# A 64-byte step between the first block of each weight piece and the rest

## The reference, cut to what matters

```python
def swiglu(h, w_in, w_out):
    gu = jnp.einsum('bld,de->ble', h, w_in)
    g, u = jnp.split(gu, 2, axis=-1)
    return jnp.einsum('blf,fd->bld', jax.nn.silu(g) * u, w_out)

# first block, per layer, for x and (but for the last layer) for the context
q, k, v, up, ca, cb = project_inputs(h, w_in[l], q_norm_g[l], k_norm_g[l])
mix = jnp.concatenate([attn, pool_o, conv_o], axis=-1)
x = x + g1 * jnp.einsum('blm,md->bld', mix, w_out[l])
x = x + g2 * swiglu(modulate(rms_norm(x, norm2_g[l]), sh2, sc2), w_ffn_in[l], w_ffn_out[l])
# second block, per layer
c_q, c_kv, k_r, q_d, k_d, v_d = jnp.split(h @ w_in[l], split_at, axis=-1)
x = x + mixed @ w_out[l]
x = x + conv_ffn(rmsnorm(x, ffn_norm[l]), w_up[l], conv_w[l], conv_b[l], w_down[l])
```

## Time and profile before

| | |
|---|---|
| median of 3 runs | 1796.46 us |
| lowest, highest | 1794.70, 1797.76 us |
| the profiled execution | 1794.97 us |
| its span, first to last instruction | 1793.1 us |
| mean granted TensorE clock | 0.977 |
| TensorE matmul busy, weight load busy | 1685.8 us (94%), 1526.0 us (85%) |
| VectorE, ScalarE, GpSimd busy | 1063.0 us (59%), 886.3 us (49%), 192.7 us (11%) |
| weights and other input read | 296.10 MB, mean 166 GB/s |

### The profile page before, as it was taken

The page is one execution under the profiler, slowest core; times in us unless marked ns, Lnnn a source line. Parts: engine busy times, 40 slices in busy tenths (PEclk is TensorE's granted clock), DMA queues, the critical chain, the costliest instruction groups (busy, mean ns, idle before and its releaser), DMA issues. The chain is left out here.

```text
span 1793.1 us, 30262 instructions
## 1 busy us (share of the span) xinstructions
PE 1685.8 (94%) x12864; PEld 1526.0 (85%) x12864; DVE 1063.0 (59%) x1472; ACT 886.3 (49%) x1192; POOL 192.7 (11%) x138
## 2 busy tenths in 40 slices
PE   5899988999999999997999999988999999889999
PEld 2777666999999999965899989757999987679999
DVE  2498657644445444986644445755776456657773
ACT  3334555544345434555544335655555366556552
POOL 1140000122003210300022100000011000000110
PEclk7899999999999999999999999999999999999999
DMA  9233646466446545363266453302555533025553
GB/s 368 94 141 136 240 165 216 184 235 252 171 165 211 185 174 182 141 238 138 99 221 201 172 174 130 132 22 86 186 184 194 177 120 134 24 95 184 184 195 119
DMA packets 45110, 299.12 MB, mean 167 GB/s; under 512 B 5216, under 2 KB 7360, under 8 KB 11696
## 3 DMA queue, kind: packets, MB, share of 16 engines
q1 hardware_dynamic: 44304, 295.65, 46.0%
q0 software_dynamic: 240, 0.79, 0.1%
q10 hardware_dynamic: 432, 0.75, 0.1%
HBM read 296.10 MB, written 1.06 MB: 166 GB/s over the span
## 5 line engine op out<-in xcount | busy, mean ns | idle before, releaser
L1749 DVE TENSOR_TENSOR wl<-raw,wh 128x2048 fp32r<-128x2048 f32 (+3 forms) x236 | 529.0, 2242 | 520.8 <-ACT wh L1523 470.0
L1523 ACT ACTIVATE wh<-raw 128x2048 fp32r<-128x2048 f32 (+3 forms) x236 | 436.8, 1854 | 259.4 <-PE bank L1334 158.8
L1329 PE MATMUL bank<-hx_hi,wh 128*128 128x256 f32 x1920 | 547.9, 285 | 16.3 <-ACT hx_hi L1523 9.7
L1332 PE MATMUL bank<-hx_hi,wl 128*128 128x256 f32 x1920 | 539.8, 281 | 3.3 <-DVE wl L1749 3.3
L1334 PE MATMUL bank<-hx_lo,wh 128*128 128x256 f32 x1920 | 540.4, 281 | 0.0
L1329 PEld LDWEIGHTS bank<-hx_hi,wh 128*128 128x128 f32 x1920 | 364.0, 190 | 23.9 <-issue 19.7
L1332 PEld LDWEIGHTS bank<-hx_hi,wl 128*128 128x128 f32 x1920 | 364.3, 190 | 8.8 <-DVE wl L1749 4.6
L1334 PEld LDWEIGHTS bank<-hx_lo,wh 128*128 128x128 f32 x1920 | 363.8, 189 | 0.5 <-DVE hx_lo L1741 0.2
L1332 PE MATMUL bank<-hid_hi,wl 128*128 128x256 f32 x880 | 245.4, 279 | 0.5 <-DVE wl L1749 0.5
L1334 PE MATMUL bank<-hid_lo,wh 128*128 128x256 f32 x880 | 245.4, 279 | 0.0
L1329 PE MATMUL bank<-hid_hi,wh 128*128 128x256 f32 x880 | 245.3, 279 | 0.0
(11 more groups left out here) (208 smaller groups left out, 1955.0 us busy)
## 6 DMA issues: line engine op xcount, KB each, us to landing
raw<-in_wts SPq DMA_DIRECT2D x258, 1024.0 KB, 4.8
raw<-in_wts SPq DMA_DIRECT2D x20, 768.0 KB, 4.0
raw<-in_wts SPq DMA_DIRECT2D x4, 576.0 KB, 3.5
tmp<-tscr SPq DMA_DIRECT2D x16, 128.0 KB, 4.3
raw<-in_wts SPq DMA_DIRECT2D x2, 640.0 KB, 3.9
xTc<-in_ctxT SPq DMA_DIRECT2D x1, 1024.0 KB, 10.8
xTx<-in_xT SPq DMA_DIRECT2D x1, 1024.0 KB, 8.6
out_x<-xTx POOLq DMA_DIRECT2D x3, 256.0 KB, 5.5
```

The source lines that it names most:

```text
L1329: pe.matmul(out, hi[:, k, c:c + m], x_hi, start=first and k == 0 and o == 0, stop=False, skip_group_check=True)
L1332: pe.matmul(out, lo[:, k, c:c + m], x_hi, start=False, stop=False, skip_group_check=True)
L1523: return act.activation(out, in_, func, bias=bias, scale=scale)
L1749: tt(M.wl[k][:, 0:ne], M.raw[f["r"]][:, 0:ne], M.wh[k][:, 0:ne].bitcast(F32), ALU.subtract).then_inc(*on.inc(f["tlo"]))
```

## The change

Every piece whose operands are read block by block gets 16 columns of zeros (64 bytes) behind its first block. `wh` and `wl` start at a multiple of 128 bytes. Block 0 thus starts at a multiple of 128, and every later block 64 bytes behind one, as all blocks did before. `mod` and `ukv` pieces get no step and so lie at multiples of 128 throughout. A slot grows to 2064 columns, 8256 bytes. The eight small tensors `st` (32 bytes each) move into the 64-byte gaps that alignment leaves between the `wh` and `wl` buffers. The three `raw` buffers lie behind each other without alignment, so the middle one now starts 64 bytes behind a multiple of 128. The loads, the splits by ScalarE and VectorE and the input array carry the 16 columns along. The matmuls are the same in number, order and shape; they never read the zeros.

```diff
+STEP = 16
-SLOT = 2048
+SLOT = 2048 + STEP
...
-        keys += [(("up1", l, j), SLOT) for j in range(22)]
+        keys += [(("up1", l, j), 2048, 256) for j in range(22)]
...
-    return {k: (i, n) for i, (k, n) in enumerate(keys)}
+    return {k: (i, n + STEP if first else n, first) for i, (k, n, first) in enumerate(keys)}
...
         def align(at):
-            cur[0] += (at - cur[0]) % 256
+            cur[0] += (at - cur[0]) % 128
...
-        align(192)
-        self.wh = [sb(f"wh{i}", [P, SLOT], F32R) for i in range(NSPLIT)]
-        self.wl = [sb(f"wl{i}", [P, SLOT], F32R) for i in range(NSPLIT)]
+        self.wh, self.wl, self.st = [], [], []
+        for i in range(2 * NSPLIT):
+            align(0)
+            w, name = ((self.wh, "wh"), (self.wl, "wl"))[i % 2]
+            w.append(sb(f"{name}{i // 2}", [P, SLOT], F32R))
+            if i < 4:
+                self.st += [sb(f"st{2 * i + j}", [P, 8]) for j in range(2)]
...
+    def block(w, k, ncols, c, m):
+        at = k * ncols + (STEP if k else 0) + c
+        return w[:, at:at + m]
...
-                pe.matmul(out, hi[:, k, c:c + m], x_hi, start=first and k == 0 and o == 0, stop=False,
+                pe.matmul(out, block(hi, k, ncols, c, m), x_hi, start=first and k == 0 and o == 0, stop=False,
...
-                pe.matmul(out, a[0][:, k, sl], hi[:, k, :], start=k == 0 and j == 0, stop=False, skip_group_check=True)
+                pe.matmul(out, a[0][:, k, sl], block(hi, k, 256, 0, 256), start=k == 0 and j == 0, stop=False, skip_group_check=True)
...
     def put(key, a):
-        row, n = PT[key]
-        out[row, :, 0:n] = a
+        row, n, first = PT[key]
+        if first:
+            out[row, :, 0:first], out[row, :, first + STEP:n] = a[:, 0:first], a[:, first:]
+        else:
+            out[row, :, 0:n] = a
```

More of the change, by code:

```diff
@@ L31, in piece_table @@
         for cb in range(3):
-            keys += [(("mod", l, cb, k), SLOT) for k in range(8)]
-        keys += [(("in1", l, j), SLOT) for j in range(9)]
-        keys += [(("out1", l, kh, ch), SLOT) for kh in range(2) for ch in range(2)]
-        keys += [(("up1", l, j), SLOT) for j in range(22)]
-        keys += [(("dn1", l, ch, kb), (2048, 2048, 1536)[kb]) for ch in range(4) for kb in range(3)]
-    for l in range(2):
[L38 to L43, removed]
-    return {k: (i, n) for i, (k, n) in enumerate(keys)}
+            keys += [(("mod", l, cb, k), 2048, 0) for k in range(8)]
+        keys += [(("in1", l, j), 2048, 256) for j in range(9)]
+        keys += [(("out1", l, kh, ch), 2048, 512) for kh in range(2) for ch in range(2)]
+        keys += [(("up1", l, j), 2048, 256) for j in range(22)]
+        keys += [(("dn1", l, ch, kb), (2048, 2048, 1536)[kb], 256) for ch in range(4) for kb in range(3)]
+    for l in range(2):
+        keys += [(("in2", l, 2), 1280, 160) if j == 2 else (("in2", l, j), 2048, 256) for j in range(9)]
+        keys += [(("uq", l, j), 1152, 384) for j in range(2)]
+        keys += [(("ukv", l), 2048, 0)]
+        keys += [(("out2", l, kh, ch), 2048, 512) for kh in range(2) for ch in range(2)]
+        keys += [(("up2", l, j), 2048, 256) for j in range(22)]
+        keys += [(("dn2", l, ch, kb), (2048, 2048, 1536)[kb], 256) for ch in range(4) for kb in range(3)]
+    return {k: (i, n + STEP if first else n, first) for i, (k, n, first) in enumerate(keys)}
 def vec_table():
@@ L199, in __init__ @@
         self.nlam = sb("nlam", [P, 2])
-        self.st = [sb(f"st{i}", [P, 8]) for i in range(8)]
         self.tmp = [sb(f"tmp{i}", [P, 512]) for i in range(8)]
@@ L286, in dma @@
             r = n % NRAW
-            row, ne = self.PT[self.pieces[n]]
+            row, ne, _ = self.PT[self.pieces[n]]
             t = self.ev(f"raw{r}", 16)
@@ L1318, in tensor_program @@
 def tensor_program(pe, on, M, plan):
+    def block(w, k, ncols, c, m):
+        at = k * ncols + (STEP if k else 0) + c
+        return w[:, at:at + m]
     def gemm(f, nk, ncols, tiles, a, a_toks, k0, first, last, free, t, **_):
-        hi = M.wh[f["k"]][:, 0:nk * ncols].rearrange("p (k c) -> p k c", k=nk)
-        lo = M.wl[f["k"]][:, 0:nk * ncols].rearrange("p (k c) -> p k c", k=nk)
+        hi, lo = M.wh[f["k"]], M.wl[f["k"]]
         for k in range(nk):
@@ L1328, in gemm @@
                     on.wait_ge(free[j])
-                pe.matmul(out, hi[:, k, c:c + m], x_hi, start=first and k == 0 and o == 0, stop=False,
+                pe.matmul(out, block(hi, k, ncols, c, m), x_hi, start=first and k == 0 and o == 0, stop=False,
                           skip_group_check=True)
                 on.wait_ge(f["tlo"])
-                pe.matmul(out, lo[:, k, c:c + m], x_hi, start=False, stop=False, skip_group_check=True)
+                pe.matmul(out, block(lo, k, ncols, c, m), x_hi, start=False, stop=False, skip_group_check=True)
                 on.wait_ge(a_toks[k0 + k][1])
-                ins = pe.matmul(out, hi[:, k, c:c + m], x_lo, start=False, stop=last and k == nk - 1,
+                ins = pe.matmul(out, block(hi, k, ncols, c, m), x_lo, start=False, stop=last and k == nk - 1,
                                 skip_group_check=True)
@@ L1338, in gemm_tok @@
     def gemm_tok(f, nk, b, free, a, a_toks, t, **_):
-        hi = M.wh[f["k"]][:, 0:nk * 256].rearrange("p (k c) -> p k c", k=nk)
-        lo = M.wl[f["k"]][:, 0:nk * 256].rearrange("p (k c) -> p k c", k=nk)
+        hi, lo = M.wh[f["k"]], M.wl[f["k"]]
         on.wait_ge(free, f["thi"])
@@ L1345, in gemm_tok @@
                 on.wait_ge(a_toks[k][0])
-                pe.matmul(out, a[0][:, k, sl], hi[:, k, :], start=k == 0 and j == 0, stop=False, skip_group_check=True)
+                pe.matmul(out, a[0][:, k, sl], block(hi, k, 256, 0, 256), start=k == 0 and j == 0, stop=False, skip_group_check=True)
                 on.wait_ge(f["tlo"])
-                pe.matmul(out, a[0][:, k, sl], lo[:, k, :], start=False, stop=False, skip_group_check=True)
+                pe.matmul(out, a[0][:, k, sl], block(lo, k, 256, 0, 256), start=False, stop=False, skip_group_check=True)
                 on.wait_ge(a_toks[k][1])
-                ins = pe.matmul(out, a[1][:, k, sl], hi[:, k, :], start=False, stop=k == nk - 1, skip_group_check=True)
+                ins = pe.matmul(out, a[1][:, k, sl], block(hi, k, 256, 0, 256), start=False, stop=k == nk - 1, skip_group_check=True)
         ins.then_inc(*on.inc(t))
@@ L1461, in mla_k1 @@
     def mla_k1(hp, f, b, free, ck_toks, t, **_):
-        whi, wlo = (x[f["k"]][:, :].rearrange("p (k c) -> p k c", k=2) for x in (M.wh, M.wl))
+        whi, wlo = (x[f["k"]][:, 0:2048].rearrange("p (k c) -> p k c", k=2) for x in (M.wh, M.wl))
         on.wait_ge(free, f["thi"], f["tlo"])
```

## The result

The changed kernel takes 1783.32 us (median of 4 runs, 1781.76 to 1784.55) beside 1797.11 us before (4 runs): ratio 0.9918, 95% interval 0.9905 to 0.9931, 13.8 us less. The profiled execution took 1783.53 us, its span is 1781.6 us; against the 1794.97 us of before, that is 11.4 us less. The prediction had 1767 us.

The account below looks back on a forecast made before the run. TensorE's pace of starting matmuls in the long stages was taken as the bound. 1794.97 - 25.2 - 5.5 + 1.0 = 1765.3 us for the profiled execution, 1766.8 at the median, rounded to 1767; range 1753 to 1811.

Parts of the forecast that it names:

- The rule on SBUF: TensorE's operand reads: by the skill page no address could change the matmul pace, the change slightly slower for its columns.
- the first rival: Matmul pace: addresses don't matter or nudges cancel, leaving 1 us for the columns, 1797.5 us; no effect within 0.2%, chance 0.14.
- The step as a nudge: Entry to each piece and after block 0: the address shift leads long-paced matmuls into the short pace; 30.7 us won.
- second rival: Entry into block 1: nudge brings the long pace, 5.9 us lost, block 0 slower, 7 us; 1810 us, chance 0.28.
- The third rival: Split pieces: the step works only in part, for instance not behind stalls; half of 30.7 us, 1782 us, chance 0.13.
- The 28.8 us for 2180 triples at full effect: Saturated long-paced stages: each group of three matmuls shortens by 0.0132 us; 25.2 us won with block 0 left long.
- Block 0 was charged with the long pace: First block of each piece: assumed to stay at the long pace, so 28.8 x 7/8 = 25.2 us.
- The short-paced pieces: Stretches already at the short pace, 446 triples: no loss in the main sum, 5.9 us lost if all turned long.
- The mixed stages: Stages with attention and modulation among projections, 948 triples: half of 12.5 x 7/8, 5.5 us won.
- The columns: Splits and loads carrying 16 more columns: 14 ns on ScalarE, 18 ns on VectorE; together 1 us lost, range 0 to 3.
- The DMA rule: Loads at a pitch of 8256 bytes: misaligned rows cost 261 beats on the mean instead of 256, hidden at DMA share 0.5.
- The cover: Feeding of TensorE at the shorter pace, 5.44 us a piece: loads and splits keep up, nothing becomes late.

Follow-up runs that it names:

- e1_front: Changed kernel with the zeros moved ahead of block 0, so no step within a piece; 1776.76 us, ratio 0.9876 to the kernel before.
- e2_zero: Changed kernel with the zeros moved behind the piece, so all blocks of split pieces lie at multiples of 128; 1817.86 us, ratio 1.0104 to the kernel before.
- f3_step: Changed kernel with alignment kept modulo 256: the step in the old layout, small tensors filling gaps; 1804.22 us, ratio 1.0039 to the kernel before.
- g2_distance: Kernel before with only the three `wh` buffers moved, by 128 bytes down, to 64 modulo 256; 1774.37 us, ratio 0.9874.
- g1_both: Kernel before, no zeros, with activations moved to 128 and `wl` to 64 modulo 256, `wh` staying at 192; 1772.76 us, ratio 0.9857.
- g4_distance_same: Kernel before with activations staying at 0 and `wh` and `wl` both at 64 modulo 256; 1779.83 us, ratio 0.9896.
- g3_turned: Kernel before with activations at 128, `wh` at 64 and `wl` at 192 modulo 256; 1785.71 us, ratio 0.9945.
- f1_halves: Kernel before with `wl` alone moved by 128, to 64 modulo 256, `wh` staying at 192; 1789.59 us, ratio 0.9946.
- f2_moving: Kernel before with the activations alone moved from 0 to 128 modulo 256; 1778.00 us, ratio 0.9894.

## Why the prediction failed in its main step and held in others

**What bounds the kernel.** Right: the pace in the long stages. Addresses alone moved the time from 1776.76 us in `e1_front` to 1817.86 in `e2_zero`, which have the same work, loads and splits.

**The rule on SBUF.** The Trainium skill, "SBUF — State Buffer", section "SBUF: two separate sides", has it that TensorE never waits on anyone in SBUF, by which no address would matter (the first rival, 1797.5). The measurements say otherwise: 1.0104 in `e2_zero` and 0.9876 in `e1_front`, which differ only in where the weights lie within the same buffers. The page may mean waits on other engines only. Whether it is reads of TensorE against each other, no run shows.

**The step as a nudge.** This is what failed. The prediction had the step lead the stream from the long pace into the short one at equal addresses. `f3_step`, the step alone, does the opposite: +7 us. And in the new layout it costs 6.6 us (`e1_front`). Its second rival described the step alone: the short stretches are gone. Its price was too high, 5.9 + 7 us and 1 for the columns against 7 measured in all.

**The sign and the number.** That the kernel got faster as forecast, though by 13.8 us and not by 29, is luck: the forecast had it from the step, and it came from the layout. The third rival had 1782 us for a partial effect, close to the measured 1783.32, and that is luck too. It had the step work in some pieces and fail in those behind a stall. In the long stages of the trace every piece, behind a stall or not, has the short pace in its bulk and pays at its entry.

**What was overlooked.** The sentence that everything "keeps its remainder modulo 128" was true and the wrong question. `align` modulo 128 moves the activations by 128 modulo 256 and sets `wh` and `wl` 128 apart. That side effect is the whole gain: it makes the distance pair (64, 192), at which only the short pace lasts. `g2_distance` makes the same pair by moving `wh` alone.

**The size of the terms.** The 28.8 us for 2180 triples at full effect are right for the pace alone: `g1_both`, with the short pace throughout, gains 27.3 in its even distances. Its stages get only 19.5 shorter. Block 0 was charged with the long pace in 2 of 16 triples, 0.026 us a piece; it costs 0.079, as the passage reaches into block 2. That makes 0.132 x 2180 / 16 = 18.0 us instead of 25.2. The even distances show 17.7 and the stages 12.9. The 4.9 us between them go at waits and at the lower clock, 2.0 of them from 300 to 350 us; one by one the rest isn't assigned. The short-paced pieces, at 0 in the forecast, lose 0.079 x 446 / 16 = 2.2 us, and the three stages show 2.2. The mixed stages were to bring 5.5 us and brought 0.9 with the columns in it; even `g1_both`, with neither step nor columns, gets only 3.6 there. Half of their ceiling was too much: other engines and the clock (0.97 to 0.95 from 696 to 875 us) set the time there. 12.9 - 2.2 + 0.9 is 11.6, and 0.1 is lost from 885 to 896 us: 11.4 us (unrounded), the difference of the profiled executions.

**The columns.** Right: 15 and 17 ns a split where 14 and 18 were expected. A `ukv` piece has 60 matmuls where the prediction said about 72, a term that it took as nothing either way.

The DMA rule of the Trainium skill, "DMA: Bandwidth & Descriptors", section "How a descriptor splits into AXI transactions", would make the loads at a pitch of 8256 bytes slower. The prediction's estimate from that page, 261 beats instead of 256, would be 4.85 us instead of 4.76. The trace agrees: the same 208 pieces land in 4.76 us before and 4.85 after, in 4.84 and 4.83 in `e1_front` and `e2_zero` with that pitch, and in 4.76 and 4.74 in `g1_both` and `g2_distance` without it. About half of the 0.09 us is the 0.8% of longer rows, and no run parts the two. As the prediction had it, it stays hidden for the most part. `e1_front` and `g1_both`, with the same distances, differ by 4 us, but their intervals overlap and the `raw` buffers lie differently; how much of it is the columns stays open.

**The cover.** "Nothing becomes late" was wrong. The long stages are mostly fed, but the waits for `wl` grow from 13.9 to 17.5 us, and with the clock behind them this takes back the 4.9 us above, 7.8 in `g1_both`. The sum had no term for it.

## What to carry to other kernels

When a matmul stream runs at two paces with the same shapes and clock, compare the addresses of its stationary and moving operands modulo 256, and not only modulo 128, and try a few distances; it costs only a change of alignment. Read in a diff every tensor that an alignment rule moves, not only the one it is meant for. Undo each half of a change alone: here the intended half cost 7 us and a side effect won 20.

## What the runs showed of the hardware

- With fp32r tiles of 128 by 128 as weights and 256 moving columns, neighbouring `gemm` matmuls start 113.3, 117.7 or about 119 ns apart at a clock of 1.00. Which of these last depends on the distance modulo 256 between weights and activations: only the short pace at (64, 192) (`g1_both`, `g2_distance`, 92% and 91% short), two patterns at (192, 64), (64, 64) and (192, 192), only the slowest at (0, 128) (`e2_zero`, 0%). Turning all places by 128 bytes changed nothing beyond the intervals in three pairs of kernels.
- The order matters: (64, 192) and (192, 64) differ by 11 us on the one side (`g2_distance`, `g3_turned`) and 17 on the other (`g1_both`, `f1_halves`). Why is open, as is the mechanism as a whole; the pairs (0, 0), (128, 0) and (128, 128) were not tried throughout a piece.
- Single executions of one kernel spread by 18 to 23 us in 8 to 10 of them for three kernels with two lasting patterns (`f1_halves`, `g3_turned`, `g4_distance_same`), and by 2 to 6 us in 4 of them where only one lasts (`e1_front`, `e2_zero`, `g1_both`, `g2_distance`). It isn't a rule: `f2_moving`, also with two patterns, spread by 6 us in 4, and the kernel before by 8 in 21.
- A gap of 2.24 us between two starts was followed by 16 matmuls at 1.2 GHz (`g1_both`), one of 1.86 us at the same point was not (before), and neither was one of 2.27 us there (`g4_distance_same`). In the kernel after, one of 2.13 us was and one of 2.16 us elsewhere was not. So the gap alone doesn't decide.
